# Reordering the last eight units ahead of the output projection: gate and branch products in turn

## The reference, cut to what matters

```python
for l in range(DEPTH):                                   # 2
    u = rms_norm(x, norm1_w[l])
    proj = u @ w_in[l]                                   # conv, GLA, attention inputs, and 3 x 1024 gates
    ya, yb, yc = short_conv(...), gla(...), swa(...)     # three branches, 512 wide each
    branch = jnp.einsum('bsgc,gcd->bsgd', ybr, w_branch[l])
    gate = jax.nn.sigmoid(gates.reshape(Bsz, S, 3, D))
    mixed = jnp.sum(gate * branch, axis=2)
    x = x + mixed @ w_o[l]
    h = rms_norm(x, norm2_w[l])
    x = x + jnp.square(jax.nn.relu(h @ w_up[l])) @ w_down[l]
```

## Time and profile before

| | |
|---|---|
| median of three runs | 1582.59 us |
| the profiled execution, its own time | 1582.82 us |
| its span, first to last instruction | 1581.0 us |
| TensorE busy (matmul) | 1559.6 us, 99% |
| VectorE busy | 1040.2 us, 66% |
| ScalarE busy | 771.9 us, 49% |
| GpSimd busy | 107.0 us, 7% |
| granted TensorE clock | 0.999 |
| split high, 128x1024 (ACT) | 1060 ns each |
| split low, 128x1024 (DVE) | 1225 ns each |

### The profile page before, as it was taken

One profiled execution on the slowest core, in us unless ns is written; L12 is line 12 of the kernel. 1 busy time (PEld: TensorE's weight loads), 2 busy tenths in 40 slices (PEclk: granted clock), 3 DMA queues, 4 the chain that ended last, 5 costly groups with the idle time before them and its releaser, 6 DMA issues.

```text
span 1581.0 us, 21301 instructions
## 1 busy us (share of the span) xinstructions
PE 1559.6 (99%) x7480; PEld 1273.5 (81%) x7480; DVE 1040.2 (66%) x1487; ACT 771.9 (49%) x1163; POOL 107.0 (7%) x92
## 2 busy tenths in 40 slices
PE   8999999999999999999999999999999999999998
PEld 7877778888778888888787777788887788888886
DVE  5577774555686757586866777655457676665778
ACT  5547552322456364546445566432235473636362
POOL 0000000000121011111100000000002111101010
PEclk9999999999999999999999999999999999999999
DMA  6321224532396665747323212155324855656553
GB/s 230 108 81 54 83 78 147 170 109 84 87 217 156 166 145 145 175 109 207 61 81 99 89 55 80 54 169 178 107 80 96 237 120 173 146 169 138 137 130 94
DMA packets 131210, 199.38 MB, mean 126 GB/s; under 512 B 6528, under 2 KB 82848, under 8 KB 131104
## 3 DMA queue, kind: packets, MB, share of 16 engines
q1 hardware_dynamic: 106448, 151.27, 28.8%
q0 software_dynamic: 23936, 46.14, 17.5%
q10 hardware_dynamic: 720, 0.61, 0.1%
HBM read 170.74 MB, written 2.10 MB: 109 GB/s over the span
## 4 chain that ended last, share of the span: by engine, by line
PE 83%; DVE 9%; ACT 2%; DVEq 2%; DMA 2%; issue 1%; SPq 0%; ACTq 0%
PE acc L566 19%; PE acc L567 18%; PE acc L568 18%; PE acc L629 5%; PE acc L630 5%; PE acc L631 5%; DVE wl_rows L1145 3%; PE acc L588 3%; PE acc L590 2%; PE acc L589 2%; DVE x_tokens L1508 1%; DMA x_tokens<-product_sums 1%; PE bank L766 1%; PE bank L785 1%; PE bank L777 1%
## 5 line engine op out<-in xcount | busy, mean ns | idle before, releaser
L566 PE MATMUL acc<-uh,wh 128*128 128x512 f32 x1152 | 453.5, 394 | 4.2 <-DVEq L1239 3.3
L568 PE MATMUL acc<-uh,wl 128*128 128x512 f32 x1152 | 449.2, 390 | 0.0
L567 PE MATMUL acc<-ul,wh 128*128 128x512 f32 x1152 | 449.1, 390 | 0.0
L566 PEld LDWEIGHTS acc<-uh,wh 128*128 128x128 f32 x1152 | 216.6, 188 | 56.7 <-issue 7.1
L568 PEld LDWEIGHTS acc<-uh,wl 128*128 128x128 f32 x1152 | 216.7, 188 | 45.9
L567 PEld LDWEIGHTS acc<-ul,wh 128*128 128x128 f32 x1152 | 216.8, 188 | 43.6
L1145 DVE TENSOR_TENSOR wl<-raw,wh 128x1024 fp32r<-128x1024 f32 x142 | 174.0, 1225 | 98.1 <-ACT wh L859 85.5
L859 ACT ACTIVATE wh<-raw 128x1024 fp32r<-128x1024 f32 x142 | 150.5, 1060 | 143.7 <-PE acc L568 88.7
L859 ACT ACTIVATE wh_rows<-raw_down 128x1024 fp32r<-128x1024 f32 x140 | 148.5, 1061 | 122.5 <-PE acc L631 90.9
L1145 DVE TENSOR_TENSOR wl_rows<-raw_down,wh_rows 128x1024 fp32r<-128x1024 f32 x140 | 171.5, 1225 | 23.3 <-ACT wh_rows L859 11.3
L1024 ACT ACTIVATE gate_tanh<-gate_tanh 128x512 f32<-128x512 f32 x40 | 25.3, 633 | 171.7 <-DVEq L1176 171.7
(11 more groups left out here) (260 smaller groups left out, 2439.5 us busy)
## 6 DMA issues: line engine op xcount, KB each, us to landing
raw<-in_w_in_dram SPq DMA_DIRECT2D x39, 1024.0 KB, 5.2
raw<-in_w_up_dram SPq DMA_DIRECT2D x32, 1024.0 KB, 6.2
raw_down<-in_w_down_dram SPq DMA_DIRECT2D x32, 1024.0 KB, 8.4
raw_down<-raw_down POOLq DMA_DIRECT2D x40, 512.0 KB, 5.8
raw_down<-in_w_down_dram POOLq DMA_DIRECT2D x32, 512.0 KB, 6.2
raw_branch<-in_w_in_dram SPq DMA_DIRECT2D x12, 1024.0 KB, 5.0
raw_branch<-in_w_branch_dram SPq DMA_DIRECT2D x12, 1024.0 KB, 5.1
raw_down<-in_w_o_dram SPq DMA_DIRECT2D x8, 1024.0 KB, 8.4
```

Of the source, the lines that this page charges most:

```text
L566: nc.tensor.matmul(a[:], wh[slot][:, k, :], right_h, start=at_k == 0, stop=False)
L567: nc.tensor.matmul(a[:], wh[slot][:, k, :], right_l, start=False, stop=False)
L568: last = nc.tensor.matmul(a[:], wl[slot][:, k, :], right_h, start=False, stop=at_k == n - 1)
```

## The change

The last eight units of each layer's gates change their order from gate20 gate21 gate22 gate23 br20 br21 br22 br23 to gate20 gate21 br20 gate22 br21 gate23 br22 br23. This holds for the order on TensorE, ScalarE and VectorE, for `split_ahead`, and for the loads: the branch slab is now loaded before the slab of gate22 and gate23. The first third of `ACT_LATE` and `DVE_LATE` is written anew. Slab numbers and the place in a slab no longer come from the place in `LAYER`, but from the unit's own number.

```diff
-GATES = [f"{kind}{8 * g + 4 * half + i}" for g in range(N_BRANCH) for half in range(2)
-         for kind in ("gate", "br") for i in range(4)]
+LAST_HALF = (("gate", 0), ("gate", 1), ("br", 0), ("gate", 2), ("br", 1), ("gate", 3), ("br", 2), ("br", 3))
+def gate_steps(g, half):
+    steps = LAST_HALF if half and g == N_BRANCH - 1 else [(kind, i) for kind in ("gate", "br") for i in range(4)]
+    return [(kind, 8 * g + 4 * half + i) for kind, i in steps]
+GATES = [f"{kind}{i}" for g in range(N_BRANCH) for half in range(2) for kind, i in gate_steps(g, half)]
...
-ACT_LATE = """wc0 +wo3 wc1 +wo4 wc2 +wo5 wc3 +wo6 wh1 wh2 +wo7 +wo8 wh3 wc4 +wo9 wc5 +wo10 +wo11 +wo12 +wo13 +up0 +up1 V0 V1 V2 V3
-+up2 V4 sq0 V5 +up3 V6 sq2 V7 rl0 +up4 hh0 rl1 sq1 sq3 +up5 +up6 rl2 rl3 +up7 hh1 rl4 hh2 +dn0 hh3 +dn1 rl5 sh0 dh0
+ACT_LATE = """+wo3 wc0 wc1 +wo4 +wo5 +wo6 wc2 wh1 +wo7 wh2 wc3 +wo8 +wo9 wc4 wh3 wc5 +wo10 +wo11 +wo12 +wo13 +up0 V0 V1 +up1 V2 V3
++up2 V4 V5 +up3 sq0 V6 sq2 V7 +up4 rl0 +up5 rl1 hh0 sq1 sq3 +up6 hh1 rl2 rl3 +up7 rl4 +dn0 hh2 hh3 hh4 sh0 rl5 +dn1
...
-DVE_LATE = """+wo3 +wo4 ws +wo5 +wo6 wl1 wl2 +wo7 wl3 +wo8 wr7 wr6 +wo9 wf1 wf4 +wo10 +wo11 wr8 wr9 +wo12 +wo13 wr10 wr11 +up0 V0 V1
-wr12 V2 V3 wr13 +up1 +up2 V4 +up3 V5 V6 V7 +up4 RM +up5 +up6 hl0 df0 +up7 su0 hl1 hl2 +dn0 +dn1 su1 sl0 dl0 su2 hl3
+DVE_LATE = """+wo3 +wo4 ws +wo5 +wo6 wl1 wl2 +wo7 +wo8 +wo9 wr6 wr7 wf1 +wo10 wr8 wl3 wr9 +wo11 +wo12 wf4 wr10 wr11 +wo13 +up0 V0 V1
+wr12 V2 V3 wr13 +up1 V4 +up2 V5 +up3 V6 V7 +up4 hl0 +up5 +up6 RM df0 hl1 su0 hl2 +up7 +dn0 hl3 sl0 +dn1 su1 hl4 dl0
...
-    elif UNIT[_u] % 2:
-        SLAB[_u] = SLAB[LAYER[UNIT[_u] - 1]]
+    elif _i % 2:
+        SLAB[_u] = SLAB[f"{_kind}{_i - 1}"]
...
-                        for i in range(first, first + 4, 2):
-                            load(l, f"gate{i}", rows(w_in, l, 0, KT, COL["gates"] + i * P, SLAB_COLS))
-                        load(l, f"br{first}", w_branch[...], raw4[SLAB[f"br{first}"] % 2][:])
+                        for kind, i in gate_steps(g, half):
+                            if kind == "gate" and i % 2 == 0:
+                                load(l, f"gate{i}", rows(w_in, l, 0, KT, COL["gates"] + i * P, SLAB_COLS))
+                            elif kind == "br" and i == first:
+                                load(l, f"br{i}", w_branch[...], raw4[SLAB[f"br{i}"] % 2][:])
```

More of the change, by code:

```diff
@@ L91 @@
 up31 dn42 dn43 dn44 dn45 dn46 dn47 dn48 dn49 dn50 dn51 dn52 dn53 UT4 UT5 UT6 UT7 dn54 dn55""".split()
-ACT_LATE = """wc0 +wo3 wc1 +wo4 wc2 +wo5 wc3 +wo6 wh1 wh2 +wo7 +wo8 wh3 wc4 +wo9 wc5 +wo10 +wo11 +wo12 +wo13 +up0 +up1 V0 V1 V2 V3
-+up2 V4 sq0 V5 +up3 V6 sq2 V7 rl0 +up4 hh0 rl1 sq1 sq3 +up5 +up6 rl2 rl3 +up7 hh1 rl4 hh2 +dn0 hh3 +dn1 rl5 sh0 dh0
-rl6 sh1 +dn2 hh4 +dn3 sh2 +dn4 rl7 +dn5 sh3 +dn6 hh5 +dn7 +dn8 hh6 +dn9 +dn10 hh7 +dn11 +dn12 +dn13 +up8 +up9 rl8
+ACT_LATE = """+wo3 wc0 wc1 +wo4 +wo5 +wo6 wc2 wh1 +wo7 wh2 wc3 +wo8 +wo9 wc4 wh3 wc5 +wo10 +wo11 +wo12 +wo13 +up0 V0 V1 +up1 V2 V3
++up2 V4 V5 +up3 sq0 V6 sq2 V7 +up4 rl0 +up5 rl1 hh0 sq1 sq3 +up6 hh1 rl2 rl3 +up7 rl4 +dn0 hh2 hh3 hh4 sh0 rl5 +dn1
+dh0 +dn2 rl6 +dn3 sh1 sh2 +dn4 rl7 +dn5 sh3 +dn6 hh5 +dn7 +dn8 hh6 +dn9 +dn10 hh7 +dn11 +dn12 +dn13 +up8 +up9 rl8
 +up10 hh8 rl9 hh9 +up11 +up12 rl10 +up13 hh10 rl11 +up14 rl12 +up15 dh1 +dn14 hh11 rl13 hh12 sh4 +dn15 hh13 sh5 +dn16
@@ L103 @@
 UT6 UT7""".split()
-DVE_LATE = """+wo3 +wo4 ws +wo5 +wo6 wl1 wl2 +wo7 wl3 +wo8 wr7 wr6 +wo9 wf1 wf4 +wo10 +wo11 wr8 wr9 +wo12 +wo13 wr10 wr11 +up0 V0 V1
-wr12 V2 V3 wr13 +up1 +up2 V4 +up3 V5 V6 V7 +up4 RM +up5 +up6 hl0 df0 +up7 su0 hl1 hl2 +dn0 +dn1 su1 sl0 dl0 su2 hl3
-sl1 +dn2 hl4 +dn3 sl2 +dn4 rs1 rs0 su3 sl3 +dn5 +dn6 rs2 hl5 rs3 +dn7 rs5 +dn8 rs4 hl6 +dn9 hl7 rs7 rs6 +dn10 +dn11
+DVE_LATE = """+wo3 +wo4 ws +wo5 +wo6 wl1 wl2 +wo7 +wo8 +wo9 wr6 wr7 wf1 +wo10 wr8 wl3 wr9 +wo11 +wo12 wf4 wr10 wr11 +wo13 +up0 V0 V1
+wr12 V2 V3 wr13 +up1 V4 +up2 V5 +up3 V6 V7 +up4 hl0 +up5 +up6 RM df0 hl1 su0 hl2 +up7 +dn0 hl3 sl0 +dn1 su1 hl4 dl0
+su2 +dn2 +dn3 sl1 sl2 rs0 rs1 +dn4 su3 sl3 +dn5 +dn6 rs2 hl5 rs3 +dn7 rs5 +dn8 rs4 hl6 +dn9 hl7 rs7 rs6 +dn10 +dn11
 rs9 rs8 +dn12 +dn13 rs10 +up8 +up9 rs11 rs12 rs13 +up10 hl8 +up11 +up12 +up13 hl9 df1 +up14 hl10 su4 dl1 +up15 +dn14
@@ L391, in slab_ends @@
             kind, i = step_of(u)
-            return i % 4 == 3 if kind == "br" else UNIT[u] % 2 == 1
+            return i % 4 == 3 if kind == "br" else i % 2 == 1
         def use_of(l, u):
@@ L413, in raw_view @@
                 return raw4[slot][:, :, i % 4 * P:i % 4 * P + P]
-            return raw[slot][:, :, UNIT[u] % 2 * P:UNIT[u] % 2 * P + P]
+            return raw[slot][:, :, i % 2 * P:i % 2 * P + P]
         def split_view(high, u, l=0):
@@ L511, in _ @@
                         first = 8 * g + 4 * half
-                        for i in range(first, first + 4, 2):
-                            load(l, f"gate{i}", rows(w_in, l, 0, KT, COL["gates"] + i * P, SLAB_COLS))
-                        load(l, f"br{first}", w_branch[l, g, :, half * SEQ:(half + 1) * SEQ].rearrange(
-                            "(k p) n -> p k n", p=P), raw4[SLAB[f"br{first}"] % 2][:])
+                        for kind, i in gate_steps(g, half):
+                            if kind == "gate" and i % 2 == 0:
+                                load(l, f"gate{i}", rows(w_in, l, 0, KT, COL["gates"] + i * P, SLAB_COLS))
+                            elif kind == "br" and i == first:
+                                load(l, f"br{i}", w_branch[l, g, :, half * SEQ:(half + 1) * SEQ].rearrange(
+                                    "(k p) n -> p k n", p=P), raw4[SLAB[f"br{i}"] % 2][:])
                 for q in range(QUARTERS):
@@ L798, in gates @@
                     for half in range(2):
[L799 to L802, removed]
+                        for kind, i in gate_steps(g, half):
+                            if kind == "gate":
+                                if i >= first:
+                                    unit(l, f"gate{i}", u_tile)
+                                continue
                             def branches_ready():
@@ L1018, in _ @@
                     for half in range(2):
-                        first = 8 * g + 4 * half
-                        for i in range(first, first + 4):
-                            if i >= 4:
+                        for kind, i in gate_steps(g, half):
+                            if kind == "gate" and i >= 4:
                                 split_ahead(l, f"gate{i}")
@@ L1024, in _ @@
                                 nc.scalar.activation(gt[:, i % 4, :], gt[:, i % 4, :], ACT.Tanh, scale=0.5).then_inc(gate_ready, 1)
[L1025 to L1032, removed]
+                            elif kind == "br":
+                                split_ahead(l, f"br{i}")
+                                if i == 8 * N_BRANCH - 1:
+                                    act.wait_ge(unit_done, unit_at(l, f"br{i}") + 1 + UNIT_CREDIT)
+                                    sum_high(l, 0)
+                                if g == N_BRANCH - 1:
+                                    act.wait_ge(mixed_done, l * 8 + i % 8 + 1)
+                                    nc.scalar.activation(yh[:, i % 8, :], mixed[:, i % 8, :], ACT.Copy, scale=0.5).then_inc(mx_hi, 1)
                 for word in ACT_LATE:
@@ L1477, in _ @@
                         first = 8 * g + 4 * half
[L1478 to L1485, removed]
+                        for kind, i in gate_steps(g, half):
+                            if kind == "gate":
+                                if i >= 4:
+                                    V.drain()
+                                    split_ahead(l, f"gate{i}")
+                                    if final and half and i == first:
+                                        mixed_low(i % 8 - 1)
+                                    scaled_gate(l, i)
+                                continue
                             V.drain()
```

## The result

The changed kernel takes **1584.97 us**, the median of 20 runs (1583.41 to 1585.95); the kernel before, on the same chip, 1582.59 us (1582.04 to 1583.27). The ratio is 1.0014, with a 95% interval of 1.0008 to 1.002: the change costs 2.4 us. The forecast of 1580.3 us has the wrong sign, and the time lies 2.1 us above the range.

A forecast was written before the change was run, and what follows sets the result against it. TensorE bounds the kernel (busy 1559.6 of 1581.0 us), so only its stops can be won. Gains of 1.15 and 1.35 us per layer, together 2.5, less 0.2 for gate20, make 2.3: 1582.59 to 1580.3 us, range 1577.8 to 1582.9.

The forecast's parts named there:

- Part 1: New order of the eight gate and branch units: VectorE's backlog shrinks, wo2 and wo5 come 0.87 us earlier per layer.
- rival C: Before br20: gate22's slab lands late, 2.8 us lost per layer at worst, 1585.7 us; chance 0.05.
- Part 2: Output projection's new lists: stops at wo9 (0.6 us) and wo10 (1.2) go, a new one of 0.5 at wo11.
- Rival E: New feed-forward lists open a stop: 1 to 3 us slower than forecast per layer, 1583 to 1586; chance 0.07.
- Part 3: From the second right DMA to V4: part of the gain is given back, leaving 1.15 us in layer 0, 1.35 in layer 1.
- the half rate: Beside the down blocks' load, GpSimd's queue moves 0.10 MB/us instead of 0.19, slowing the second right sum.
- A: Second right DMA lands before 458.4 and is no limit; V4 moves 2.1 us per layer, 1578.4 us; chance 0.27.
- B: Earlier down load slows both last sums, landing stays at 460.4, V4 stays: 1582.6 us, no change; chance 0.12.

The follow-up runs named there:

- e4: Changed kernel, but the first buffer of down blocks is handed back one word later, behind wf4: 1579.84 us, ratio 0.998.
- e1: Changed kernel, but both buffers of down blocks are handed back only after the split of wo13: 1580.01 us, ratio 0.9983.
- e2: Kernel before, with both buffers of down blocks handed back only after the split of wo13: 1582.37 us, ratio 0.9997.
- e7: Changed kernel with 14 spare matmuls ahead of up0 in layer 0, into an unused bank: 1583.68 us, ratio 1.0006.
- e3: Kernel before, with the split of wo12 ahead of wr9, so the load is issued before the right sum: 1591.04 us, ratio 1.0054.
- e6: The new late lists with the old order of the gates, against the kernel before: 1587.30 us, ratio 1.003.
- e9: Changed kernel with each down load cut into four transfers of 0.5 MB in place of two of 1 MB: 1582.18 us, ratio 0.9997.
- e8: e4 with the split of wo11 moved ahead of wl3 on VectorE: 1580.39 us, ratio 0.9985.

## Why the prediction was wrong

**What held.** Part 1 nearly to the tenth: VectorE takes br22 at 415.42 (said: 0.3 behind TensorE's end), wo2 starts at 423.61 (said: 423.7), with a stop of 0.4, and wo5 at 432.16 (said: 432.3). gate20 costs nothing, so rival C is out: its scaled read begins at 395.13, where 396.2 was reckoned for its end. Of Part 2, the stops at wo9 and wo10 are gone, and wo11 has its new one (0.8 with the late second matmul, said: 0.5). That gain is real: once the load is out of the way (e4) it is 3.0 us for both layers, and 2.4 with the load held in both kernels (e1 against e2), against 2.5 in the sum. That V4 of layer 0 in e1 (464.33) meets the forecast's 464.35 is luck: there wr12 starts at 459.31 because VectorE's list is late, and not because of the landing. Rival E is out too, with 308 of 308 us.

**What was missed in Part 2.** "wl1 and the split of wo7 just meet TensorE." They don't. The new list puts the split of wo7 ahead of wh2 on ScalarE, and the block for it lands hardly earlier than before (at 433.5 us, before at 433.6). So wl2 (435.80) waits 1.06 us for ScalarE, and wo7 starts 0.4 us late. VectorE's list is 0.85 late from there on, and wr9 runs at 447.95 instead of "about 447.1". In layer 1 the wait is for ScalarE's word wc3, which the new list puts behind the split of wo7. The text had named this kind of miss as what would make it wrong; it costs tenths.

**What failed, in Part 3**, in three terms, each of which brings the load and the sum closer together or makes that dearer:

1. "The stream of eight sums ahead is continuous [...], so it moves by 0.87 only." Its first sum does (423.86 instead of 424.84), but the sixth waits for a split and is issued at 438.77, as before (438.78). The second left sum thus goes out at 448.56 (said: 447.9), 0.2 earlier than in the earlier trace rows.
2. "The second right one 1.2 behind it." 1.2 is the duration of the instruction in the earlier trace rows, and the prediction took it for the distance at which two can follow. The distance is 2.2: GpSimd stands 1.00 us on "issue" between them. The trace of before had such waits in its stream of sums (1.81 us on "issue" ahead of the one at 431.11), and the forecast left them out. So the sum goes out at 450.75 (said: 449.1), 1.3 earlier than before instead of 3.0.
3. "Beside that load GpSimd's queue moves 0.10 MB/us instead of 0.19." This rate was read in a window where both queues had their packets in, and it was applied to a load that starts sooner. It holds once the sum has begun; it says nothing of who begins. The load was said to follow the sum by 450.5 - 449.1 = 1.4 us and followed by 0.69, where the sum takes 12.1. At 1.4 us the second column of the table gives 8.4 to 9.0, and wr12 would have been on time. By the third column it would not: the load would be issued 2.7 us or more ahead of the left sum's landing (447.9 + 5.3), and the sum shut out even so. The term that failed is the same by both: the landing beside an earlier load, put at 10.2 us by the half rate, took 12.1, of which 3.6 were shut out.

By the Trainium skill, page "DMA: Bandwidth & Descriptors", section "Queues, rings and completion order", an engine goes round the queues that have work, a packet at a time. The trace agrees from 457 us on (49 packets against 48 from 458 to 459), but for the 3.6 us ahead of that q0 has none, although e1 shows that the sum's packets stood ready. Where the two differ the trace decides.

The 3.6 us by which wr12 is later than the forecast (462.92 against 459.35) are thus 1.65 from the issue and 1.9 from the landing. What the prediction lacked altogether is what follows on it: behind the stop ahead of up0 the clock falls, and V4 comes 6.6 us after wr12 instead of the 5.0 that was carried over from the earlier trace rows (e1 and e7: 5.0). Layer 0 therefore ends 469.53 - 464.35 = 5.2 us behind the forecast. The forecast also spread the wait over up0 and V4. But up0 opens the bank that wr12 frees, so it takes the full wait at once, and behind this one long stop the clock is at 0.50.

**The rivals.** A (the landing is no limit, 1578.4) has its condition met in e1 and e4: wr12 waits for no DMA. Yet they take 1580.0 and 1579.8 us, since wr12 is ready at 459.31 and 458.99 by VectorE's list, and not at the 458.4 that was reckoned. The changed kernel is not of this kind in layer 0, but it is in layer 1. B named the right place and the right partner, and called its worst case "no change"; the landing went 2.5 us beyond that (462.9 instead of 460.4). No rival let the landing come later than before, as none let the earlier load overtake the sum. That is the gap in the range: the chance of 0.06 for slower by over 3.2 us came from other mechanisms.

**Open**: that layer 1, with the same lists, has a distance of 1.27 and not 0.69 is read, not tested: its second left sum and its splits are shifted by tenths against each other. Which of the two measures decides, why one queue then shuts the other out, and why in e3 for 1.6 MB, isn't known.

## What to carry to other kernels

When a change brings a large load forward, work out not only how much it slows the small transfer on the path but whether it can pass it: take the distance of the two issues, and how long the load waits for the transfer that goes ahead of the small one. Treat anything closer than in the trace of before as unproved ground, with a price of its own. Where a load isn't needed soon, hold its release back behind one more instruction; here one word (1.4 us of VectorE) turned 2.4 us lost into 3.0 us won. And when a wait is moved to a new place on TensorE, add what the clock takes after it.

## What the runs showed of the hardware

- A sum of 0.5 MB from SBUF to SBUF takes 5.8 to 5.9 us alone (e1, e2), 8.2 to 9.0 beside a load that is issued 1.0 to 1.3 us behind it, and 12.1 to 12.3 beside one that is issued 0.5 to 0.7 behind it.
- While it is shut out, the other queue moves about the size of one of its transfers with 1 MB each (kernel after, e6, e7) and with 0.5 MB each (e9), but 1.6 MB in e3, where they have 1 MB too.
- The load can be shut out as well: issued 2.06 us behind the sum (e4), it had its first packets 3.7 us after its issue, instead of 1.0 us on free engines (e1).
- GpSimd can issue two such sums 0.73 us apart (438.77 and 439.50). But the second right one came 2.0 to 2.7 us behind the second left one in all runs of the new lists but e8 (where it waited for wr9), with 0.8 to 1.5 us on "issue", for which the profile names no cause.
- After a stop of 4.1 us TensorE was granted 0.50, the 1.2 GHz level (kernel after). It ran 12 matmuls at 0.43 us and was back at 1.00 by 470 us; together that cost 1.4 to 1.6 us. After a stop of 2.4 us (e9) the clock fell to 0.50 too, within the matmuls of up0 (0.40 us at 462.93, 0.63 at 463.69). With the long stop filled by spare matmuls (e7) it stayed at 1.00.
